# The chunk inverse of two delta-rule mixers, with X and y in the other partition half

## The reference

```
m = jnp.where(strict, jnp.einsum('nbhcd,nbhsd->nbhcs', k_beta, k) * decay, 0.0)
t_inv = lax.linalg.triangular_solve(eye + m, jnp.broadcast_to(eye, m.shape), left_side=True, lower=True)
u = t_inv @ v_beta
w = t_inv @ (k_beta * jnp.exp(gc)[..., None])
```

## Time and profile before

| | |
|---|---|
| median of 3 runs | 2156.62 us (2156.28 to 2156.7) |
| the profiled execution's own time | 2154.3 us |
| its span | 2152.5 us |
| TensorE busy | 2072.7 us (96%) |
| VectorE busy | 1103.5 us (51%) |
| ScalarE busy | 751.6 us (35%) |
| GpSimd busy | 737.1 us (34%) |
| mean granted TensorE clock | 0.986 |

### The profile page before, as it was taken

How to read it: one execution, slowest core, us unless ns; L and a number is a source line. 1 busy time by engine, 2 the same in 40 slices (tenths; PEclk the granted TensorE clock), 3 DMA queues, 4 the chain that set the end, 5 groups by cost and what they waited for, 6 DMA issues and landing times.

```text
span 2152.5 us, 34726 instructions
## 1 busy us (share of the span) xinstructions
PE 2072.7 (96%) x14520; PEld 1609.7 (75%) x14520; DVE 1103.5 (51%) x1820; ACT 751.6 (35%) x1152; POOL 737.1 (34%) x550
## 2 busy tenths in 40 slices
PE   5999999999999999999989999999999999999997
PEld 3778787766777888888867877877576778888886
DVE  5885554797833422222356855558967333222223
ACT  3541512344353342323243334133353434322312
POOL 1540212331223444444435222034223244444442
PEclk7999999999999999999989999999999999999998
DMA  4320111221212333223232111022113123332321
GB/s 168 98 87 16 59 32 51 86 86 50 101 47 78 112 99 96 91 97 98 90 106 83 57 36 55 23 74 91 49 47 127 54 79 98 98 91 96 98 92 65
DMA packets 52266, 170.03 MB, mean 79 GB/s; under 512 B 5648, under 2 KB 13968, under 8 KB 51600
## 3 DMA queue, kind: packets, MB, share of 16 engines
q1 hardware_dynamic: 50928, 162.75, 23.6%
q0 software_dynamic: 1184, 5.07, 0.6%
HBM read 160.45 MB, written 7.34 MB: 78 GB/s over the span
## 4 chain that ended last, share of the span: by engine, by line
PE 84%; DVE 11%; ACT 3%; issue 1%; DMA 1%; SPq 0%; DVEq 0%; ACTq 0%
PE bank_a L468 13%; PE bank_a L469 13%; PE bank_a L472 12%; PE bank_v L472 7%; PE bank_v L468 7%; PE bank_v L469 7%; PE bank_v L608 5%; PE bank_v L530 4%; PE bank_v L728 2%; DVE mg L1420 1%; DVE arena L1414 1%; PE bank_f L541 1%; PE bank_v L710 1%; PE bank_f L547 1%; PE bank_a L859 1%
## 5 line engine op out<-in xcount | busy, mean ns | idle before, releaser
L429 POOL TENSOR_TENSOR w_lo<-ring,w_hi 128x512 fp32r<-128x512 f32 x536 | 730.7, 1384 | 1295.8 <-ACT w_hi L1094 1295.7
L468 PE MATMUL bank_a<-h_hi,w_hi 128*128 128x512 f32 x1376 | 560.7, 407 | 6.9 <-DVE h_lo L1447 4.8
L469 PE MATMUL bank_a<-h_lo,w_hi 128*128 128x512 f32 x1376 | 540.1, 393 | 0.0
L1094 ACT ACTIVATE w_hi<-ring 128x1024 fp32r<-128x1024 f32 x268 | 281.5, 1050 | 234.5 <-DVE arena L1950 220.1
L472 PE MATMUL bank_a<-h_hi,w_lo 128*128 128x512 f32 x1376 | 340.8, 390 | 0.0
L468 PEld LDWEIGHTS bank_a<-h_hi,w_hi 128*128 128x128 f32 x1376 | 260.0, 189 | 88.2 <-issue 24.0
L469 PEld LDWEIGHTS bank_a<-h_lo,w_hi 128*128 128x128 f32 x1376 | 260.7, 189 | 59.8 <-issue 8.1
L472 PEld LDWEIGHTS bank_a<-h_hi,w_lo 128*128 128x128 f32 x1376 | 259.2, 188 | 54.1
L468 PE MATMUL bank_v<-parts,w_hi 128*128 128x512 f32 x640 | 254.5, 398 | 1.3 <-DVE parts L1921 1.3
L469 PE MATMUL bank_v<-parts,w_hi 128*128 128x512 f32 x640 | 253.4, 396 | 0.0
L1414 DVE TENSOR_TENSOR sg<-bank_v,sg 128x512 f32<-128x512 f32 x112 | 77.5, 692 | 326.7 <-PE bank_v L472 256.5
(11 more groups left out here) (271 smaller groups left out, 2405.4 us busy)
## 6 DMA issues: line engine op xcount, KB each, us to landing
ring<-in_w SPq DMA_DIRECT2D x268, 512.0 KB, 3.5
out_ring<-in_w SPq DMA_DIRECT2D x64, 128.0 KB, 3.5
x_dram<-arena SPq DMA_DIRECT2D x2, 2048.0 KB, 7.6
arena<-x_dram SPq DMA_DIRECT2D x2, 2048.0 KB, 9.3
arena<-in_x SPq DMA_DIRECT2D x2, 1024.0 KB, 8.4
arena<-tabs POOLq DMA_DIRECT2D x4, 512.0 KB, 4.5
out_x<-arena SPq DMA_DIRECT2D x2, 1024.0 KB, 4.6
par<-in_par POOLq DMA_DIRECT2D x2, 937.0 KB, 7.2
```

Source lines behind the costliest of these rows:

```text
L429: ins = nc.gpsimd.tensor_tensor(w_lo[:, g % SPLIT, ks, :], raw, w_hi[:, g % SPLIT, ks, :].bitcast(F32), ALU.subtract)
L468: mm(b[:], w_hi[:, s, k, :], hi[:, k, :], start=k == 0, stop=False)
L469: mm(b[:], w_hi[:, s, k, :], lo[:, k, :], start=False, stop=False)
L1094: act_fn(w_hi[:, g % SPLIT, :, :], ring[:, g % RING, :, :], ACT.Copy).then_inc(S["split_hi"], 1)
```

## The change

The inverse keeps T and U where they are and moves X and y to the other partition half (even chunks in 64 to 127, odd ones in 0 to 63).

- Start: besides the 16 products for T, each half has 16 products that copy X through the identity to the other half, into a second `bank_a` bank; ACT copies that out too (a new step, semaphore "xs").
- Y: the same 16 products for each half, results in the other partition half. These use the two corners off the diagonal.
- T and X of one level and half are issued together, one product of T and one of X in turn, into two banks. T takes only the even block columns of y, X only the odd ones of its own (`side`), so each product has 32 moving columns in place of 64 and each bank is half filled. DVE subtracts each with 256 elements a partition in place of 512.
- Last level: no T. X is brought back to its own half by accumulating identity times X and (minus y) times X in one bank: 32 products of 64 columns for each half in place of 16, all off the diagonal. DVE copies the bank in place of subtracting.
- TensorE's waits change with it: a T-and-X group waits for X, y and two banks.

The core of the diff, TensorE:

```
-            def invert(l, x, V, fill):
+            def invert(l, x, V, beside):
+                U, X, Y, TI = V["u"], V["x"], V["y"], V["t"]
+                chunks = lambda half: [(k, half * M // 2 + k, p_) for k in range(M // 2) for p_ in range(2)]
+                here, there = lambda p_: quarter(p_), lambda p_: quarter(1 - p_)
...
                 for half in range(2):
                     pe.wait_ge(S[x + "_x1"], at(l, x + "_x1", half + 1))
-                    chunk_products("a", x + "_ti", half, V["x"], lambda m, p_: cst("ident")[quarter(p_), quarter(p_)])
+                    bt, bx = bank("a", x + "_ti"), bank("a", x + "_xs")
+                    for k, m, p_ in chunks(half):
+                        eye = cst("ident")[here(p_), here(p_)]
+                        last_t = mm(bt[here(p_), k * C:(k + 1) * C], X[here(p_), m, :], eye, start=True, stop=True)
+                        last_x = mm(bx[there(p_), k * C:(k + 1) * C], eye, X[here(p_), m, :], start=True, stop=True)
...
-                        chunk_products("v", x + "_y", half, V["u"], lambda m, p_: V["t"][quarter(p_), m, :])
+                        by = bank("v", x + "_y")
+                        for k, m, p_ in chunks(half):
+                            ins = mm(by[there(p_), k * C:(k + 1) * C], U[here(p_), m, :], TI[here(p_), m, :], start=True, stop=True)
...
+                        if n == len(LEVELS) - 1:
+                            beside(half)
+                            bx = bank("v", x + "_x")
+                            pe.wait_ge(S[x + "_y"], at(l, x + "_y", 2 * n + half + 1))
+                            for k in range(M // 2):
+                                m, cols = half * M // 2 + k, slice(k * C, (k + 1) * C)
+                                for p_ in range(2):
+                                    mm(bx[here(p_), cols], cst("ident")[there(p_), there(p_)], X[there(p_), m, :], start=True, stop=False)
+                                for p_ in range(2):
+                                    ins = mm(bx[here(p_), cols], Y[there(p_), m, :], X[there(p_), m, :], start=False, stop=True)
+                            ins.then_inc(v_full, 1)
+                        else:
+                            pe.wait_ge(S[x + "_y"], at(l, x + "_y", 2 * n + half + 1))
+                            bt, bx = bank("v", x + "_t"), bank("v", x + "_x")
+                            for k, m, p_ in chunks(half):
+                                cols = slice(k * C // 2, (k + 1) * C // 2)
+                                last_t = mm(bt[here(p_), cols], X[there(p_), m, :], side(Y[there(p_), m, :], s, 0), start=True, stop=True)
+                                last_x = mm(bx[there(p_), cols], Y[there(p_), m, :], side(X[there(p_), m, :], s, 1), start=True, stop=True)
```

DVE (ACT has only the second copy of the start more):

```
-                        v.tensor_tensor(V["y"][:, ms, :], bank3(b, C), wide(f"level{s}_c"), MUL).then_inc(S[x + "_y"], 1)
+                        v.scalar_tensor_tensor(V["y"][:, ms, :], bank3(b, C), -1.0 if last else 1.0, wide(f"level{s}_c"), MUL, MUL).then_inc(S[x + "_y"], 1)
...
+                        if last:
+                            v.tensor_copy(V["x"][:, ms, :], bank3(b, C)).then_inc(S[x + "_x"], 1)
+                        else:
+                            t_ = side(V["t"][:, ms, :], s, 0)
+                            v.tensor_tensor(t_, t_, half_bank(b, s), SUB).then_inc(S[x + "_t"], 1)
+                            dve.wait_ge(v_full, filled.next())
+                            b = filled.bank()
+                            x_ = side(V["x"][:, ms, :], s, 1)
+                            v.tensor_tensor(x_, x_, half_bank(b, s), SUB).then_inc(S[x + "_x"], 1)
```

More of the change, by code:

```diff
@@ L42 @@
 LEVELS = (2, 4, 8, 16, 32)
[L43 removed]
+INVERSE_STEPS = ("x1", "ti", "xs", "y", "t", "x", "wt", "u")
 GDN0, MLA0, RWK0, DSA0, GATE0 = 0, 1032, 1448, 2472, 3824
@@ L326, in quarter, with side @@
             return slice(i * C, (i + 1) * C)
+        def side(view, s, x):
+            lead = " ".join("abc"[:len(view.shape) - 1])
+            w = view.rearrange(f"{lead} (j x i) -> {lead} j x i", x=2, i=s)
+            return w[:, :, x, :] if len(view.shape) == 2 else w[:, :, :, x, :]
         def merges_to(g):
@@ L609, in chunk_products, with bank @@
                 ins.then_inc(v_full if pool == "v" else a_full, 1)
-            def invert(l, x, V, fill):
+            def invert(l, x, V, beside):
+                U, X, Y, TI = V["u"], V["x"], V["y"], V["t"]
+                chunks = lambda half: [(k, half * M // 2 + k, p_) for k in range(M // 2) for p_ in range(2)]
+                here, there = lambda p_: quarter(p_), lambda p_: quarter(1 - p_)
+                def bank(pool, done):
+                    b, reader, emptied = banks.next(pool, done)
+                    pe.wait_ge(reader, emptied)
+                    return b
                 for half in range(2):
                     pe.wait_ge(S[x + "_x1"], at(l, x + "_x1", half + 1))
-                    chunk_products("a", x + "_ti", half, V["x"], lambda m, p_: cst("ident")[quarter(p_), quarter(p_)])
-                for n in range(len(LEVELS)):
+                    bt, bx = bank("a", x + "_ti"), bank("a", x + "_xs")
[3 more added lines that the diff above has]
+                        last_x = mm(bx[there(p_), k * C:(k + 1) * C], eye, X[here(p_), m, :], start=True, stop=True)
+                    last_t.then_inc(a_full, 1)
+                    last_x.then_inc(a_full, 1)
+                for n, s in enumerate(LEVELS):
                     for half in range(2):
@@ L625, in invert @@
                         if n:
                             pe.wait_ge(S[x + "_x"], at(l, x + "_x", 2 * (n - 1) + half + 1))
[L627 to L631, removed]
+                        else:
+                            pe.wait_ge(S[x + "_xs"], at(l, x + "_xs", half + 1))
@@ L804, in _ @@
                 pair_matrices(R["bd"], R["rt"], "r")
-                invert(l, "r", R, lambda n: None)
+                invert(l, "r", R, lambda half: None)
                 pe.wait_ge(S["r_tok"], at(l, "r_tok", 8))
@@ L844, in _ @@
                 merge_outputs(0, numbers)
-                invert(l, "g", G, lambda n: None)
+                invert(l, "g", G, lambda half: None)
                 pe.wait_ge(S["g_tok"], at(l, "g_tok", 6))
@@ L1019, in invert @@
                     act_fn(V["t"][:, half * M // 2:(half + 1) * M // 2, :], bank_m(b), ACT.Copy).then_inc(S[x + "_ti"], 1)
+                    act.wait_ge(a_full, filled.next())
+                    b = filled.bank()
+                    act_fn(V["x"][:, half * M // 2:(half + 1) * M // 2, :], bank_m(b), ACT.Copy).then_inc(S[x + "_xs"], 1)
                 for n in range(len(LEVELS)):
@@ L1463, in bank3, with half_bank @@
                 return b[:].rearrange("p (m n) -> p m n", n=n)
+            def half_bank(b, s):
+                return b[:, 0:T // 2].rearrange("p (m j i) -> p m j i", m=M // 2, i=s)
             def wide(mask):
@@ L1484, in invert @@
                 for n, s in enumerate(LEVELS):
+                    last = n == len(LEVELS) - 1
                     for ms in halves:
```

11 lines of the change are left out of this document (7 added, 4 removed).

## The result

| | median us | lowest to highest | runs |
|---|---|---|---|
| before | 2156.45 | 2155.92 to 2156.70 | 4 |
| changed | 2169.81 | 2167.35 to 2175.19 | 4 |

The ratio is 1.0066, with a 95% interval of 1.0054 to 1.0079: 13.4 us more, where 21.5 us less were forecast. The profiled execution took 2167.35 us, with a span of 2165.6 us against 2152.5, so the two traces differ by 13.1 us. The medians of the kernel before that were taken beside the experiments lie between 2155.61 and 2156.72 us, so a difference of less than about 1 us between two sets of runs says nothing.

A forecast was written before the change was run, and what follows sets the result against it. TensorE was taken to bound the kernel, busy for 96% of the span. Savings of 6.2 and 5.9 us in r and 9.5 in g, together 21.5, gave 2135 us from 2156.6; likeliest range 2130 to 2141, with faster rivals 2126 to 2144.

The forecast's parts named there:

- the end of the level: Full level of an inverse: TensorE stays the bound, DVE's 3.06 us of work being below the level's 4.0 us.
- Nothing takes it back later: After the inverses: no later work on TensorE, DVE, ACT or POOL cancels the gain of 21.5 us.
- A group costs 0.93 us: T-and-X group: 64 records at 14.5 ns on four corners, the weight load binding a corner whatever the columns.
- that rival: Fewer columns pay in full: a T-and-X group takes 0.5 us, giving 2127 us; chance 0.08.
- DVE passes of 256 elements: T and X passes on DVE: 0.42 us each, up to 0.69 with stride.
- Start of g: Start of g's inverse: the second copy group waits for a bank, so the Y products follow 1.0 us later.
- Last level: Last level of each inverse: 4.90 us from first Y pass to second X pass, after 3.96, so +0.95 us.
- Level of 4.0 us: Full level of an inverse: 4.0 us in place of 5.68, so 1.68 us less a level.
- the 80 records in a microsecond: Four-corner products in the profile before: 80 records a microsecond against 42, read as 15 ns a record against 29.
- The clock falls: Rival, in the inverses: waits lower TensorE's clock to 1.2 GHz, above 2190 us if half the time; chance 0.03.
- The four corners don't fill up: Rival, T-and-X groups: the pace stays at 29 ns a record, 1.87 us a group, +8.7 us, 2165; chance 0.07.
- The sum: Both layers: r -6.2 and -5.9 us, g -4.8 each, together -21.5 us (-1.0%).

The follow-up runs named there:

- the burst: Kernel before, with 256 extra 64x64 products on all four corners behind r's inverse of layer 0, results discarded: 2170.51 us against 2156.72, ratio 1.0064.
- the idle corners: Kernel before, with a second, discarded product beside each X product in the other corner of its row half, 160 an inverse: 2190.45 us against 2156.58, ratio 1.0157.
- the last kernel: Changed kernel without its 64 further products an inverse, with a projection unit inside each inverse in four pieces of six wide products: 2140.22 us, ratio 0.9932.

## Why the prediction was wrong

The step that failed is the end of the level: "So TensorE remains the bound: 4 groups of 0.93 and 0.27 of waiting". It priced a level by the time on the array and put the supply of its 384 instructions at nothing; that supply takes 1.5 x 3.73 = 5.6 us, and the 16 full levels measured 5.76 on average. "Nothing takes it back later" failed in part: 3.4 us of the loss lie outside the inverses and their starts. The rest, step by step:

- *A group costs 0.93 us*: right. Two T passes are 0.93 us apart. The 32 columns bring nothing; that rival is out. That the weight load is what binds a corner is still the prediction's reading: no run varied it.
- *DVE passes of 256 elements*: right, 0.42 us with the stride.
- *Start of g*: right. g's first Y pass is 2.32 us later than before in layer 0 (303.70 against 301.38) of which 1.38 is carried from r: +0.94 for the +1.0 forecast.
- *Last level*: too short. From the first Y pass to the second copy it is 191.78 - 186.57 = 5.21 us in r, layer 0, and 5.32, 5.41 and 6.47 in the others, 5.60 on average for 4.90. It has 384 instructions now, and the supply's 5.6 us fits it as it fits the others.
- *Level of 4.0 us*: wrong, 5.76. A group runs at the forecast pace as long as its instructions are there, 128 in 0.93 us. But a level has 384 before and after, one and a half transfers, 1.5 x 3.73 = 5.6 us.
- *The rows that misled*: the 80 records in a microsecond are a burst. They were read as a pace that lasts. A burst that stays within one transfer can't show what comes after it.
- *The clock falls*: given 0.03, and it did, in a milder form: one stretch of some 3.4 us in each inverse. Its price was also worked out wrong: 80 us for half the time is 40 us on top of the forecast of 2135, which gives 2175 and not "above 2190".
- *The four corners don't fill up*, the slower rival, had 2165, close to the time that came. Its mechanism, 1.87 us a group, did not occur; the time is a coincidence.
- *The sum*: its terms give -21.6 and not -21.5 us; the forecast of 2135 stays.

The sizes add up as follows. From the first Y pass to the last DVE pass the inverses are 1.31, 1.80, 1.14 and 3.33 us longer than before, 7.6 in all: the 16 full levels take 1.0 us more than before and the four last levels 6.6. For this part -23.6 was forecast: 31.2 us to explain. The stops in the four chains are 5.2, 5.5, 4.7 and 5.3 us, 20.7 together. The clock, by the four windows, took at most (0.05 x 32) + (0.06 x 27) + (0.05 x 32) + (0.07 x 26) = 6.6. The other 4 us were not itemised. Of the kernel's 13.1 us, 7.6 are thus in the inverses, 2.1 between r's inverse and g's first Y pass (0.94 and 1.19), and 3.4 lie elsewhere; those were not traced to a cause.

Could it have been seen? The numbers were in the profile of before. Its page gives queue q8 as 116 packets and 1.90 MB, 16.4 KB each, for 2 x 14520 records, about 250 a transfer. And 384 instructions in 5.68 us is 14.8 ns each, just above the 14.6 that the supply turned out to need. What the trace of before did not show is that 14.6 is a limit, since the array was just slower. The Trainium skill (Runtime: NRT & Kernel Launch, "Instruction fetch mechanics") has the blocks of 256 instructions, and says that crossing from one to the next is mostly hidden, since instructions are issued more slowly than they are filled in. The runs agree on the 256. They disagree on the hiding: in the burst 256 are issued in 2.09 us, and the next come after 3.73.

## What to carry to other kernels

Count TensorE's instructions beside its array time. In the dense stretches measured here 256 of them took 3.6 to 4.0 us, so a stretch of small products takes the larger of the two, and packing more corners helped only up to 256 / 3.73, about 69 instructions a microsecond. If a stretch is at that bound, remove instructions (a copy by identity products has as many as the real products) or lay wide products between the small ones, in pieces large enough that the switches stay few. A rate read from a burst holds only for the length of the burst.

## What was new about the hardware

- Transfers of TensorE's instructions: 256 each, one every 3.73, 3.73 and 3.89 us in the burst and every 3.57 to 3.97 in the inverse. The starts of two transfers are never closer than 3.3 us in the traces of before, of the changed kernel, of the burst and of the idle corners. What sets the 3.73 is open: in the changed kernel's trace a transfer itself is under way for 0.9 to 1.5 us, ends 1.2 to 1.6 us before TensorE resumes, and the next starts 1.0 to 1.7 us after that. Nothing was tried on it.
- Four instructions for a float32 product of 64x64: the page's counts move by just that (15032 - 14520 = 512 matmuls and as many weight loads for 256 products more), and the packets by one for each 256 instructions (116, 120, 126 in the three kernels with 0, 1024 and 2560 more).
- A piece of three products with 128x128 weights between 64x64 products costs 1.0 us (7.67 us for a level of 5.68 with two of them), where three among their like take 0.68 to 0.71.
- The granted clock fell to its lower level for some 3.4 us once in each inverse, behind a stop of 1.65 us in r, layer 0 (0.63 over 3.96 us) and of 1.26 us in g, layer 0. It did not fall behind g's stop of 1.40, nor in r, layer 0, of the kernel with filled corners, whose stops go up to 1.7 us (1.00 over 160 to 200 us). With wide products in the stops of every inverse it fell less often: at most twice in the four inverses, and not at all in the last kernel.
